# Second block's cumulative sums: a plain fp32 triangle product replaced by two fp32r products of a split softplus

## The reference, cut to what matters

```
z = einsum('bhqd,bhkd->bhqk', q_blk, kh) * scale
mask = k_pos[None, :] < q_pos[:, None]
log_keep = where(mask, log_sigmoid(-z), 0.0)
between = cumsum(log_keep, axis=3, reverse=True) - log_keep
a = where(mask, exp(log_sigmoid(z) + between), 0.0)
out = einsum('bhqk,bhkd->bhqd', a, vh)
```

## Time and profile before

| | |
|---|---|
| median of 3 runs | 1705.91 us (1704.5 to 1706.1) |
| the profiled execution's own time | 1705.99 us |
| its span, first to last instruction | 1704.2 us |
| PE busy | 1684.0 us (99%), 9730 matmul records |
| DVE busy | 1217.8 us (71%) |
| ACT busy | 1028.8 us (60%) |
| POOL busy | 693.7 us (41%) |
| granted TensorE clock, mean | 0.998 of full speed |

### The profile page before, as it was taken

The page is one execution under the profiler, slowest core; times in us unless marked ns, Lnnn a source line. Parts: engine busy times, 40 slices in busy tenths (PEclk is TensorE's granted clock), DMA queues, the critical chain, the costliest instruction groups (busy, mean ns, idle before and its releaser), DMA issues.

```text
span 1704.2 us, 26088 instructions
## 1 busy us (share of the span) xinstructions
PE 1684.0 (99%) x9730; PEld 1443.0 (85%) x9730; DVE 1217.8 (71%) x1832; ACT 1028.8 (60%) x1933; POOL 693.7 (41%) x672
## 2 busy tenths in 40 slices
PE   8999999999999999999999999999999999999998
PEld 7968888888868988889888878888898888788887
DVE  7977799958868799957664757666576647576663
ACT  5687776745687766655554657554555546575543
POOL 4154166702055167506760051764067600517640
PEclk9999999999999999999999999999999999999999
DMA  8825486575806586558656535866586675358662
GB/s 242 225 85 149 132 239 188 175 230 162 211 27 195 150 219 179 196 174 234 186 186 234 184 114 140 231 185 210 149 233 187 186 234 186 112 138 221 186 210 74
DMA packets 416352, 306.70 MB, mean 180 GB/s; under 512 B 10179, under 2 KB 369013, under 8 KB 416226
## 3 DMA queue, kind: packets, MB, share of 16 engines
q1 hardware_dynamic: 415538, 304.51, 61.5%
q0 software_dynamic: 688, 0.53, 0.2%
HBM read 303.95 MB, written 1.05 MB: 179 GB/s over the span
## 4 chain that ended last, share of the span: by engine, by line
PE 93%; DVE 3%; DMA 2%; ACT 1%; SPq 0%; issue 0%; DVEq 0%
PE bank L1536 33%; PE bank L1539 17%; PE bank L1652 9%; PE bank L1653 9%; PE bank L1654 9%; PE bank L1602 3%; PE bank L1615 2%; PE bank L1612 2%; DMA raw<-in_w_in 2%; PE bank L1826 1%; PE bank L1856 1%; DVE whl L958 1%; PE bank L1583 1%; PE bank L1807 1%; PE bank L1572 1%; PE bank L1574 1%
## 5 line engine op out<-in xcount | busy, mean ns | idle before, releaser
L958 DVE TENSOR_TENSOR whl<-raw,whl 128x1024 fp32r<-128x1024 f32 (+2 forms) x572 | 738.5, 1315 | 178.9 <-ACT whl L594 175.0
L1536 PE MATMUL bank<-hsA,whl 128*128 128x512 f32 x2368 | 757.8, 397 | 1.4 <-DVE U L968 1.4
L594 ACT ACTIVATE whl<-raw 128x1024 fp32r<-128x1024 f32 (+2 forms) x572 | 573.1, 1029 | 172.8 <-PE bank L1654 86.6
L1539 PEld LDWEIGHTS bank<-hsA,whl 128*128 128x128 f32 x2368 | 445.0, 188 | 100.6
L1539 PE MATMUL bank<-hsA,whl 128*128 128x256 f32 x2368 | 469.8, 278 | 0.0
L1536 PEld LDWEIGHTS bank<-hsA,whl 128*128 128x128 f32 x2368 | 366.8, 189 | 6.7 <-issue 2.9
L594 ACT ACTIVATE low<-bank 128x256 f32<-128x256 f32 x390 | 144.5, 376 | 274.1 <-PE bank L1536 253.2
L1401 POOL TENSOR_TENSOR HB<-CB,UB 128x256 f32<-128x256 f32 x88 | 123.2, 1400 | 338.6 <-ACT CB L597 338.0
L1652 PE MATMUL bank<-whl,hid 128*128 128x512 f32 x528 | 205.9, 390 | 0.0
L1654 PE MATMUL bank<-whl,hid 128*128 128x512 f32 x528 | 205.4, 389 | 0.0
L1653 PE MATMUL bank<-whl,hid 128*128 128x512 f32 x528 | 205.4, 389 | 0.0
(11 more groups left out here) (227 smaller groups left out, 1967.4 us busy)
## 6 DMA issues: line engine op xcount, KB each, us to landing
raw<-in_ffn_w_up SPq DMA_DIRECT2D x176, 512.0 KB, 5.2
raw<-in_ffn_w_down SPq DMA_DIRECT2D x120, 512.0 KB, 4.5
raw<-in_w_in SPq DMA_DIRECT2D x96, 512.0 KB, 5.9
raw<-in_ffn_w_gate SPq DMA_DIRECT2D x88, 512.0 KB, 4.0
raw<-in_w_out SPq DMA_DIRECT2D x32, 512.0 KB, 4.5
raw<-in_ffn_w_down SPq DMA_DIRECT2D x24, 256.0 KB, 2.9
G<-in_norm_g SPq DMA_DIRECT2D x12, 512.0 KB, 7.8
raw<-in_cmp_w SPq DMA_DIRECT2D x8, 512.0 KB, 5.5
```

The costliest lines, as they stand in the source:

```text
L594: return nc.scalar.activation(out_, in_, func, **kw)
L958: v.tensor_tensor(wlo[c_ % RING][:, x:y], raw[:, c_ % RAW, x:y], whi[c_ % RING][:, x:y].bitcast(F32), ALU.subtract)\
L1536: return mm(out_[:, 0:2 * n], whi[slot][:, at:at + P], rhs[:, 0:2 * n], start=x == 0, stop=False, **g32)
L1539: return mm(out_[:, n:2 * n], wlo[slot][:, at:at + P], rhs[:, 0:n], start=False, stop=False, **g32)
```

## The change

The softplus of each head is split on DVE in a high part (fp32r) and a low part (the rest, again fp32r), and PE multiplies both by a copy of the triangle in fp32r, in place of the one product in plain fp32. The product with -1 (`nones`) stays as it was, on the unsplit SP. The high and low parts have two places each (h % 2), so from head 2 on DVE waits, before it writes the high part, until the sums of head h - 2 are done. ACT makes the fp32r triangle once, at L = 0. `spH` lies in a part of U2 that holds nothing at that time, `spL` and `ntriR` behind `stickR`.

```
--- before.py
+++ after.py
@@ -248,7 +248,9 @@
     HB, _, hb_end = sb("HB", [P, 2, S], at=cb_end)
     identR, _, id_end = sb("identR", [P, P], F32R, at=hb_end)
     stickR, _, stick_end = sb("stickR", [P, 2, P], F32R, at=id_end)
-    assert stick_end <= hsB_end
+    ntriR, _, ntri_end = sb("ntriR", [P, P], F32R, at=stick_end)
+    spL, _, spl_end = sb("spL", [P, 2, 384], F32R, at=ntri_end)
+    assert spl_end <= hsB_end
 
     w = [ws_at]
 
@@ -271,6 +273,7 @@
     w[0] = ws_at
     U2 = ws("U2", [P, 20, S])
     V2 = ws("V2", [P, 2, 512])
+    spH = sb("spH", [P, 2, 384], F32R, at=ws_at + 8 * 4 * S)[0]
     SP = ws("SP", [P, 4, 384])
     AB = ws("AB", [P, 4, 384])
     CU = ws("CU", [P, 2, S + 2])
@@ -892,6 +895,7 @@
             ffn(0, n0 + 1)
             if L == 0:
                 f(identR[:, :], ident, ACT.Copy)
+                f(ntriR[:, :], C("ntri"), ACT.Copy)
                 for x in range(2):
                     ins = f(stickR[:, x, :], C("stick"), ACT.Copy)
                 ins.then_inc(stick_in, 1)
@@ -1338,7 +1342,12 @@
 
             def softplus(h):
                 dve.wait_ge(ln_ready, 8 * L + h + 1)
-                v.tensor_tensor(SP[:, h % 4, :], z_bank(h)[:, 0:384], SP[:, h % 4, :], ALU.max).then_inc(sp_ready, 1)
+                s_, hi = SP[:, h % 4, :], spH[:, h % 2, :]
+                seq.link(v.tensor_tensor(s_, z_bank(h)[:, 0:384], s_, ALU.max))
+                if h >= 2:
+                    dve.wait_ge(cum_ready, 8 * L + h - 1)
+                seq.link(v.tensor_copy(hi, s_))
+                v.tensor_tensor(spL[:, h % 2, :], s_, hi.bitcast(F32), ALU.subtract).then_inc(sp_ready, 1)
 
             def heads_lo(s):
                 dve.wait_ge(stick_hi, 4 * L + s + 1)
@@ -1912,7 +1921,8 @@
             def sums(h):
                 b_, s_ = z_bank(h), SP[:, h % 4, :]
                 pe.wait_ge(sp_ready, done + h + 1)
-                mm(b_[:, 0:S + P], C("ntri"), s_, start=False, stop=False, **g32)
+                mm(b_[:, 0:S + P], ntriR[:, :], spH[:, h % 2, :], start=False, stop=False, **g32)
+                mm(b_[:, 0:S + P], ntriR[:, :], spL[:, h % 2, :], start=False, stop=False, **g32)
                 mm(b_[:, P:S], nones[:, :], s_[:, S:S + P], start=False, stop=True, **g32).then_inc(cum_ready, 1)
 
             def values(s):
```

## The result

The change makes the kernel slower: 1715.59 us, median of 4 runs (1713.88 to 1718.37), against 1705.2 for before (4 runs, 1704.49 to 1706.1). The ratio is 1.0063, 95% interval 1.005 to 1.0076. The forecast was 1713.5 with a range from 1709.0 to 1717.5. The profiled execution took 1715.94 us, with a span of 1714.2.

The account below looks back on a forecast made before the run. The prediction took PE as the bound, with attention a relay between PE, DVE and ACT; 6.9 + 3.0 - 5.4 - 0.15 - 0.6 = 3.75 us a layer, 7.5 for two, gave 1713.5 us, range 1709.0 to 1717.5.

Parts of the forecast that it names:

- DVE's added work, 7 x 0.98: Attention, seven softpluses on DVE: link waits 0.06, cast 0.38, subtraction 0.54, together 0.98 us a head, 6.9 us a layer.
- Waits for POOL, 3.0: Heads 0 to 4: nine DVE casts and subtractions each wait 0.33 us for POOL, 3.0 us a layer, ends 0 and 5.0.
- Idle time filled, 5.4: DVE between softplus(0) and softplus(6): five idle gaps absorb 5.4 us a layer of the added work.
- The gain of 0.6 behind sums(6): PE at the attention's end: sums(6) and sums(7) give back 0.30 us each, 0.6 us a layer.
- The sum, 3.75 a layer: Attention, from softplus(0) to sums(6): 6.9 + 3.0 - 5.4 - 0.15 - 0.6 = 3.75 us slower a layer, 7.5 for two.
- POOL does not disturb: Rival: DVE's casts and subtractions don't wait for POOL; 1.85 us a layer, 1709.7 us; chance 0.18.
- Dearer instructions: Rival: cast at 0.55 us, worst POOL waits or slower fp32r products; 1715.9, 1717.6 or 1714.7 us; chance 0.14.
- PE's saving wins: Rival: DVE's additions fit its idle time, deciding below 0.88 us a head; -1.25 us a layer, 1703.5 us; chance 0.06.
- Priced at nothing: Costs taken as hidden: POOL held up perhaps 1 to 2 us, ACT's copy to ntriR some 0.3 us if uncovered.
- The signs in the profile: Expected after: products 0.18 us apart, DVE nearly never idle, PE waiting about 1.5 us more before sums(0), also later.
- Some 3.7 us later within each layer: PE, first product behind values(3): expected to start some 3.7 us later within each layer.
- The 6.6 us a layer: By the skill's exclusive-lock rule, nine DVE instructions would each lose a whole 0.73 us POOL instruction; not used in the sum.

Follow-up runs that it names:

- experiment 8: Changed kernel with 15, 9 and 6 unread products on PE ahead of sums(0), sums(5) and sums(6): 1711.83 us, ratio 1.0041.
- experiment 4: Changed kernel with 24, 16 and 10 unread products on PE ahead of sums(0), sums(5) and sums(6): 1711.92 us, ratio 1.0044.
- experiment 6: Changed kernel, POOL's convolution replaced by copies after head 4's minimum, plus 9, 9 and 6 unread products in PE's waits: 1708.17 us, ratio 1.0015.
- experiment 1: Changed kernel without DVE's split: one rounded copy feeds both fp32r products, so sums are wrong: 1703.11 us, ratio 0.9985 to before.
- experiment 9: Changed kernel with the split for heads 1, 2 and 7 only, the others as before: 1703.24 us, ratio 0.9993 to before.
- experiment 10: Split for heads 1, 2 and 7 only, their product with -1 also as two fp32r products: 1703.25 us, ratio 0.999 to before.
- experiment 2: Changed kernel with DVE's split kept but PE back to the one plain fp32 product: 1713.75 us, ratio 1.0054 to before.
- experiment 5: Changed kernel, POOL's convolution and scale split replaced by one copy per channel half after head 4's minimum: 1710.63 us, ratio 1.0032.
- experiment 3: Changed kernel, POOL's convolution and scale split replaced by one product per channel half, which landed on head 3: 1713.49 us, ratio 1.0051.
- experiment 7: Kernel before, with POOL's convolution replaced by copies after head 4's minimum: 1705.38 us, ratio 1.0001.

## Why the prediction was right, and where it was not

The forecast was a loss of 7.5 us. The medians differ by 10.4, and the range held them, in part by luck: its upper end, 1717.5, was the price of the worst waits for POOL, which did not come, and it happened to have room for the low clock, which no term priced. One of the four runs (1718.37) lies above it. Term by term:

- **DVE's added work, 7 x 0.98.** Right: 0.98 us a head. The cast takes 0.36, not 0.38, the subtraction 0.56, not 0.54, and the cast starts 0.03 us after its softplus, so the wait on `cum_ready` is free, as priced.
- **Waits for POOL, 3.0.** The step said nine instructions, 0.33 each, and that the cast might wait too. In experiment 8, at full clock, nine wait, 3.05 us in all. In the profile of after it is eight and 2.3 us: behind the first low stretch head 4's cast comes 13.4 us after softplus(0) and not 12.3, and POOL is done by then. (In experiment 4, at full clock, it is eight and 2.4 too, since there the cast of head 3 just misses POOL.) The mean of 0.34 against 0.33 is luck, since 0.33 was picked between 0 and 0.56 without a working.
- **Idle time filled, 5.4.** In experiment 8 softplus(6) starts 17.06 us behind softplus(0), in before 13.93. The six heads ahead of it added 5.9 + 3.05, of which 3.1 arrive, so 5.8 were hidden, 0.4 more than the five gaps I counted.
- **The gain of 0.6 behind sums(6).** Right at full clock. sums(6) starts 18.65 us behind softplus(0) in experiment 8 and 14.63 in before, 4.0 later, and the step of the whole attention is 3.4.
- **The sum, 3.75 a layer.** At full clock 3.4 (experiment 8), and 3.7 in experiment 4, whose first fillers ended 0.7 us late.
- **The missing term: the clock.** The prediction read "at full clock" in the earlier trace rows and took every duration of PE from there, while it forecast waits of PE of 1.5 us and more. With the waits filled the low stretches were gone (experiments 4, 6 and 8). In after softplus(6) starts 18.08 us behind softplus(0), and sums(6) 19.67, which is 1.0 us more than in experiment 8, although POOL held DVE up 0.7 us less. That is the first low stretch, on tile B, behind which DVE waits at 1011.24. sums(6) is 5.04 us late, and the whole attention 5.80: behind sums(6) the loss grows by 0.8 where 0.6 should come back, 1.4 for the second stretch. Together 2.4 us a layer, 4.7 for both.

So the profiled run comes 4.1 us above the forecast (11.6 against 7.5), 4.7 for the clock less 0.6 by which the sum was too high. The medians stand closer, 2.9 above the forecast. The stretches seem to differ between executions, of which only the first has a trace: the four runs of after have mean clocks of 0.995, 0.998, 0.995 and 0.997, for 1715.94, 1713.88, 1718.37 and 1715.24 us, and one stretch of 3.4 us at half clock is 0.001 of a mean.

**The rivals.** "POOL does not disturb" was given 1.85 us a layer. Its condition was false, but its price was near: with POOL really away a layer costs 1.7. So POOL's 3.05 us of waits put 1.7 on the end, and the rest must be hidden in DVE's idle time. "Dearer instructions" names a range that holds the measured time, and still it is refuted: neither cast, subtraction nor product was dearer. A median inside its range is no evidence for it; the durations are what it was about. "PE's saving wins" fell at the point that it named, 0.98 against 0.88 us a head; experiments 1, 9 and 10 show that the saving exists where DVE isn't the late one.

**Priced at nothing.** The copy to ntriR cost nothing: after is 1.38 us ahead of before at 798 us, ahead of the copy, and still 1.38 at 993. POOL's last result comes 1.4 us later, counted from softplus(0) (1015.49 - 1002.33 against 1015.43 - 1003.71), within the 1 to 2 given, and hidden.

**The signs in the profile.** Products 0.18 us apart, PE waiting 1.7 us more ahead of sums(0) (1.78 against 0.11), waits at sums(5), values(1) and sums(6), less than 2 us idle on DVE: all seen. "Some 3.7 us later within each layer" was 5.8 in the profile, and 3.4 to 3.7 with the clock held.

**What stays open.** Which waits bring the low clock and which do not. 1.78 us before sums(0) did in both layers of after and in one of experiment 2, and not in the other; behind waits of 1.10 and 1.26 us in L = 1 of experiment 5 nothing fell. The three longest waits were filled together, and not each by itself. Nor is it known how often each stretch comes in the executions that left no trace.

## What to carry to other kernels

Where a change makes an engine wait that runs at full clock, the wait isn't the whole price: add the chance that the work behind it runs at half clock, here 0.8 to 1.4 us for each stretch of 3.4 (0.8 in experiment 3, 3.48 against 2.69; 1.35 in experiment 2; 1.0 and 1.4 in after), and look at the granted clock of short windows before taking time for a wrong duration. Work moved to an engine with 55% idle time costs from the first instruction if the other engine already waits for it there; apply such a trade head by head, where the waiting goes the other way, as experiments 9 and 10 do, for a gain of 0.9 us a layer. To read an effect of 1 us in a run of 1700, compare the distance between two instructions on either side of it and not the whole time.

## What the runs showed of the hardware

**The granted clock falls inside and behind short waits.** In after it went to 1.2 GHz at 1004.4 us, 1.6 us into PE's wait of 1.78, and at 1021.5, within a wait of 0.82 that followed ones of 1.25 and 0.63. In experiment 2 it went at 1005.1, 1.3 us after a wait of 1.77 had ended (at 1003.83), with PE at work. In experiments 3 and 5 it went at 1021.1 and at 1018.6, at the end of a wait of 0.63 and 0.5 us after one, each behind a wait of 1.25. Over the eight attentions with the split on DVE and the waits left in (after and experiments 2, 3 and 5), five had low stretches, seven in number; over the six with the waits filled (experiments 4, 6 and 8) there was none. The ten attentions of before and of experiments 1, 7, 9 and 10, where PE waits 0.64 us at most, had none either. If five low attentions fell at random on those fourteen, they would all miss the six filled ones in 3 cases of 100, and over all twenty-four they would all fall on the eight in about 1 case of 1000. So the waits bring them, but not each time. It isn't the whole story of the low clock: outside the attentions before and some others have a stretch of their own, like the one at 475 us.

**DVE waits for POOL up to 0.15 us before the end of POOL's instruction, and then runs its full time.** Five instructions of POOL's timeline in after:

```profile
1002.84 0.48 POOL L1513 TENSOR_SCALAR U<-CU,vecT 128x256 f32<-128x256 f32 x1
1003.41 0.72 POOL L1514 TENSOR_TENSOR U<-U 128x256 f32<-128x256 f32 x1
...
1005.79 0.73 POOL L1511 TENSOR_TENSOR CU<-U 128x256 f32<-128x256 f32 x1
1006.61 0.48 POOL L1512 TENSOR_SCALAR U<-CU,vecT 128x256 f32<-128x256 f32 x1
...
1009.34 0.92 POOL L1516 TENSOR_TENSOR U<-U 128x256 f32<-128x256 f32 x1
```

The first cast starts at 1002.91. POOL ends at 1003.32; 0.15 before that is 1003.17, and 0.36 more is 1003.53, where the cast ends (1002.91 + 0.63 = 1003.54). The subtraction from 1003.57 comes out as 1004.13 - 0.15 + 0.56 = 1004.54 in the same way, the cast from 1005.98 as 1006.52 - 0.15 + 0.36 = 1006.73, the subtraction from 1006.76 as 1007.09 - 0.15 + 0.56 = 1007.50. All sixteen waits of after and all eighteen of experiment 8 fit within 0.01 us, and so does the one of 0.96 in experiment 3. It goes the other way too: POOL's sum at 1009.34, 0.73 us elsewhere, took 0.92, while DVE's subtraction of head 2 ran to 1009.65.

So the cast, with one input, waits like the subtraction, which the earlier trace rows could not tell. The waits could have been priced from POOL's timetable, where I took a mean of 0.33. The Trainium skill, "SBUF — State Buffer", section "SBUF: two separate sides", speaks of an exclusive lock that whoever comes first holds for its whole instruction. By that rule the trace agrees in kind. The 6.6 us a layer that the prediction worked out from it took the longest possible wait for all nine, an arrival at the very start of an instruction of 0.73. In experiment 8 DVE arrived 0.07 to 0.3 us into instructions of 0.48 to 0.85, was let go 0.15 before their ends, and paid 3.05. The softpluses, with their input in PSUM, stay at 541 to 559 ns in after, as in the earlier trace rows.

**A product of 128 columns in fp32r takes 0.11 us where many stand in a row** (2.79 us for 24 in experiment 4), much more than a third of the 0.175 for 384. In experiment 8 each of them has a weight load of its own, and these loads start 0.11 us apart too, so the loads may be what sets the pace; no run separates the two. In experiment 10 the first of a pair was followed after 0.06, and the pooled products behind it after 0.11.
